# The transposes of the convolution's state, moved behind the first two weight tiles' products in two dense stages

## The reference, cut to what matters

```python
def conv_ffn(xn, prev, w_up, w_gate, conv_w, conv_b, w_down):
    h = xn @ w_up
    g = xn @ w_gate
    hp = jnp.concatenate([prev.astype(h.dtype), h], axis=1)
    hc = lax.conv_general_dilated(hp, conv_w.astype(hp.dtype)[:, None, :], window_strides=(1,), padding='VALID',
                                  dimension_numbers=('NWC', 'WIO', 'NWC'), feature_group_count=D_FF) + conv_b
    return (jax.nn.gelu(hc) * g) @ w_down, hp[:, -(CONV_W - 1):]
```

## Time and profile before

| | us |
|---|---|
| median of 3 runs (lowest to highest) | 3202.26 (3201.84 to 3204.47) |
| the profiled execution, its own time | 3207.11 |
| span of the profiled execution | 3205.3 |
| PE busy | 2954.8 (92% of the span) |
| DVE busy | 1442.0 (45%) |
| ACT busy | 944.4 (29%) |
| POOL busy | 742.1 (23%) |

### The profile page before, as it was taken

One profiled execution on the slowest core, in us unless ns is written; L12 is line 12 of the kernel. 1 busy time (PEld: TensorE's weight loads), 2 busy tenths in 40 slices (PEclk: granted clock), 3 DMA queues, 4 the chain that ended last, 5 costly groups with the idle time before them and its releaser, 6 DMA issues. The chain is left out here.

```text
span 3205.3 us, 51177 instructions
## 1 busy us (share of the span) xinstructions
PE 2954.8 (92%) x19701; PEld 2833.1 (88%) x19701; DVE 1442.0 (45%) x3259; ACT 944.4 (29%) x1692; POOL 742.1 (23%) x526
## 2 busy tenths in 40 slices
PE   7988996759999799999999999989789999999998
PEld 6987886449998499999999999968689999999998
DVE  4517773446776344431442443157644441441441
ACT  4213444335554132110211123047432110210211
POOL 1124552002111132221221224232132222221221
PEclk9998998757999899999999999979889999999999
DMA  6223552032000521111111111110021111111112
GB/s 175 80 86 114 158 158 63 1 71 108 2 1 23 242 63 40 46 46 46 46 48 44 52 42 44 41 42 1 14 63 34 52 46 46 46 46 46 46 48 72
DMA packets 270117, 195.93 MB, mean 61 GB/s; under 512 B 56388, under 2 KB 260286, under 8 KB 263407
## 3 DMA queue, kind: packets, MB, share of 16 engines
q1 hardware_dynamic: 262859, 143.19, 15.7%
q0 software_dynamic: 6912, 50.33, 4.4%
q10 hardware_dynamic: 184, 0.20, 0.0%
HBM read 176.64 MB, written 24.42 MB: 63 GB/s over the span
## 5 line engine op out<-in xcount | busy, mean ns | idle before, releaser
L590 PE MATMUL ps<-xf_hi,w_hi 128*128 128x344 f32 x2352 | 757.8, 322 | 9.9 <-POOL w_lo L581 9.9
L592 PE MATMUL ps<-xf_hi,w_lo 128*128 128x344 f32 x2352 | 754.3, 321 | 0.0
L591 PE MATMUL ps<-xf_lo,w_hi 128*128 128x344 f32 x2352 | 753.6, 320 | 0.0
L581 POOL TENSOR_TENSOR w_lo<-w_raw,w_hi 128x1024 fp32r<-128x1024 f32 (+1 forms) x162 | 384.9, 2376 | 1471.9 <-ACT w_hi L577 1471.9
L590 PEld LDWEIGHTS ps<-xf_hi,w_hi 128*128 128x128 f32 x2352 | 444.0, 189 | 11.3 <-issue 11.2
L591 PEld LDWEIGHTS ps<-xf_lo,w_hi 128*128 128x128 f32 x2352 | 443.9, 189 | 0.7 <-issue 0.7
L592 PEld LDWEIGHTS ps<-xf_hi,w_lo 128*128 128x128 f32 x2352 | 444.1, 189 | 0.0
L590 PE MATMUL ps<-hid_hi,w_hi 128*128 128x344 f32 x1056 | 339.8, 322 | 0.0
L592 PE MATMUL ps<-hid_hi,w_lo 128*128 128x344 f32 x1056 | 338.0, 320 | 0.0
L591 PE MATMUL ps<-hid_lo,w_hi 128*128 128x344 f32 x1056 | 337.3, 319 | 0.0
L577 ACT CAST w_hi<-w_raw 128x1024 fp32r<-128x1024 f32 (+1 forms) x162 | 165.6, 1022 | 388.8 <-PE ps L592 384.0
(11 more groups left out here) (565 smaller groups left out, 5381.8 us busy)
## 6 DMA issues: line engine op xcount, KB each, us to landing
w_raw<-in_ffn_w_up_dram SPq DMA_DIRECT2D x44, 512.0 KB, 3.7
w_raw<-in_ffn_w_gate_dram SPq DMA_DIRECT2D x44, 512.0 KB
w_raw<-in_ffn_w_down_dram SPq DMA_DIRECT2D x32, 448.0 KB, 3.5
w_raw<-in_ffn_w_down_dram SPq DMA_DIRECT2D x16, 512.0 KB, 3.6
w_raw<-in_a_w_in_dram SPq DMA_DIRECT2D x14, 512.0 KB, 3.8
w_raw<-in_c_w_in_dram SPq DMA_DIRECT2D x10, 512.0 KB, 3.9
residual<-hT SPq DMA_DIRECT2D x1, 4128.0 KB
hT<-residual SPq DMA_DIRECT2D x1, 4128.0 KB, 17.3
```

The lines of the kernel that those rows point to most:

```text
L581: pool.tensor_tensor(self.parts.lo[:, slot, 0:kt, :], self.raw[:, slot, 0:kt, :], self.parts.hi[:, slot, 0:kt, :].bitcast(F32), ALU.subtra ...
L590: pe.matmul(psum, w_hi, x_hi, start=(a == 0), stop=False)
L591: pe.matmul(psum, w_hi, x_lo, start=False, stop=False)
L592: ins = pe.matmul(psum, w_lo, x_hi, start=False, stop=(a == kt - 1))
```

## The change

The wait for `state_rows` and the 22 transposes leave their place ahead of job 0 on PE and stand behind job 1, ahead of job 2. The other engines' programs keep every row and every wait. From there on the line numbers of the kernel after are two higher (L965 is L967 there), and the transposes are L775.

```diff
-            pe.wait_ge(s_state, 16)
-            for f in range(KF):
-                ins = pe.transpose(k.ps[:, 6, f * 16:(f + 1) * 16], state_rows[:, f * P:(f + 1) * P], k.ident[0:16, 0:16])
-            ins.then_inc(s_stp, 1)
             for j in range(KD):
                 job(j, j % 2, os, KD, (s_ol, KD, KD) if j == 0 else None)
+                if j == 1:
+                    pe.wait_ge(s_state, 16)
+                    for f in range(KF):
+                        ins = pe.transpose(k.ps[:, 6, f * 16:(f + 1) * 16], state_rows[:, f * P:(f + 1) * P],
+                                           k.ident[0:16, 0:16])
+                    ins.then_inc(s_stp, 1)
```

## The result

The changed kernel took 3215.36 us (median of 7 runs, 3211.79 to 3222.89), the kernel before 3201.84 us (7 runs, 3196.80 to 3204.47): slower by 0.46%, ratio 1.0046 with a 95% interval of 1.0036 to 1.0057, which is 11.5 to 18.3 us. The profiled execution took 3214.49 us. Forecast were 3220.5 us and a range from 3213 to 3226.

The account below looks back on a forecast made before the run. PE was taken to set the pace in the dense stages, other engines hidden behind it. Head -3.28, transposes +2.5, wait +14.2, clock +4.8 gave +18.2 us on 3202.26: 3220.5 us, range 3213 to 3226.

Parts of the forecast that it names:

- The wait: Ahead of job 2: DVE's copy waits for the moved transposes, so PE waits 7.1 us a layer, 14.2 in all.
- The head: Start of the dense stages: job 0 starts 2.48 and 0.80 us earlier without transposes ahead, 3.28 us gained.
- a rise that had stayed in time: Head of the stages: if the clock rose at the same time as before, the gain would be 1.8 us.
- The transposes: Behind job 1, at the high clock: 1.26 us a layer on PE's path, 2.5 us in all.
- halving: Transposes behind job 1: their 2.52 us at the low clock level halved to 1.26 us a layer.
- The clock: Behind the new pause: job 2 starts at the low level, products 0.287 us apart, 4.8 us lost in all.
- The second rival: Ahead of job 2: the pause comes but the clock doesn't fall, 13.4 us slower, 3215.7 us; 10%.
- the third: Job 2 runs wholly at the low level, 9.4 us a layer in place of 2.4, 3234 us; 5%.
- The first rival: Ahead of job 2: the chain stays hidden beside job 1, only the head's gain is left, some 3201.5 us; 3%.
- the chain: From transposes' end through DVE's copy, additions, ACT's parts and POOL's low part to PE's job 2: 7.1 us a layer.
- The sum: Whole kernel: -3.28 + 2.5 + 14.2 + 4.8 = +18.2 us, to 3220.5 us, 0.57% slower.
- DVE's idle time: DVE idle between its last `os_lo` and the copy of the state for some 15 us.

Follow-up runs that it names:

- the wait alone: Kernel before, transposes still at the head; only DVE waits for job 1's last product ahead of its copy of the state: 3216.76 us, ratio 1.0052.
- the pause filled: Changed kernel with 36 more products into an unused bank behind the transposes, ahead of job 2: 3212.79 us, ratio 1.0031.
- the head filled: Kernel before with transposes behind job 0, 7 or 10 fp32 products ahead of it, and 28 products in the up tile's pause: 3196.99 us, ratio 0.9981.

## Why the prediction was right

**The wait.** The step on which all hung, that DVE's copy takes job 0's additions behind job 1 and so tile 2's weights out of job 1's shade, is shown three ways: the wait alone makes the pause, the copy moved behind the additions unmakes it, and the transposes moved one job earlier unmake it too. Its size was 6.67 us a layer against 7.1, at the lower end of what the prediction allowed. The difference is in the rows: the three hand-offs, transposes to copy, `xf_hi` to `xf_lo` and POOL to PE, took 0.03 or 0.04 us each in place of 0.14, and POOL's low part 2.35 us in place of the 2.46 of the earlier trace rows.

**The head.** 2.57 and 0.89 us against 2.48 and 0.80: right, and larger by the same short hand-off. The low stretch that followed was 6.19 and 4.40 us in the change, against 4.7 and 5.9 before by the same measure (first product to the first one that is short again). That the two sums are the same is luck in part: the second profile of the change had 3.9 and 4.4, the other two of before 5.0 and 5.0, and 3.5 and 5.0. The means, 4.7 and 4.9 us, speak for a gain that was whole, as chosen; a rise that had stayed in time would have made the stretches 1.7 us longer on the mean. The kernel without transposes agrees.

**The transposes.** 1.53 us in the trace for 22, some 1.6 with the start behind job 1's last product, against 1.26 by halving. Two starts in the trace are 0.062 us apart at the high level and 0.107 at the low: it is not a half, and the rest is at the ends of the row. The estimate of 2.35 us by the Trainium skill ("TensorE: Matmul & The Clock Gate", LDWEIGHTS: columns over 1.2) was the farther one at the high level; at the low level the trace agrees with it, 22 x 0.107 = 2.35 us between starts and 2.52 for the whole row.

**The clock.** It fell in the pause, as expected. The low stretches behind it were 3.04 and 5.55 us in the first profile, 5.03 and 5.56 in the second, against 4.9 and 5.6: 3.9 or 4.8 us lost where 4.8 were counted. The second rival, a clock that doesn't fall, is out by the rows, and by them alone: its 3215.7 us lies within 1.1 us of both medians, 3215.36 and 3214.64, and the forecast of 3220.5 lies 5 to 6 us above them. The products 0.287 us apart behind the pause decide, and the 1.4 and 1.6 us that the stages lost with the pause filled; the third, a job 2 wholly at the low level (72 x 0.287 = 20.7 us), is out by the rows, too. The first rival would need the chain hidden, which only the two kernels did that undo the wait.

**The sum.** By the profiles 17.6 us in the stages, with +18.2 forecast; by the runs 14.7 and 12.2, with intervals that reach to 18.3 and 16.3. The forecast's size is at the upper end. That the range held the time owes something to its width: the prediction took 2.6 us as the spread of runs, from three, where 23 runs of before spread over 18. The terms that were too large are the chain (0.9 us in both layers) and, in one profile, the clock (0.9); the transposes were too small by 0.7. And the sum had no term for the low stretch behind the up tile's pause, which came out shorter in these profiles, by 1.2 us of time. The rest of the difference between forecast and runs isn't traced to a row.

**DVE's idle time** was put at some 15 us and was 18.3 and 17.5.

## What to carry to other kernels

Ahead of moving work on one engine, look at what stands behind its consumer in another engine's program: here one copy on an in-order queue stood ahead of all additions, and the additions were what freed the banks, and what ACT's program waited for before it rounded the next weights. A chain that is hidden has a length (here 6.7 us) and a cover, the work of PE that runs beside it (here job 1, 11.3 us). The move is free as long as the cover still lies ahead (one job earlier it did), and costs the whole chain, not the difference, once the cover is spent. When PE has a pause that can't be removed, products into an unused bank kept the clock up here; they paid where they ended before the pause did and nothing else was late next.

## What the runs showed of the hardware

PE's clock fell during 88 transposes that ran without a break: granted clock 1.00, 0.69, 0.50 and 0.50 in four stretches of 2 us in layer 0, PE busy 2.00, 2.00, 2.00 and 1.87 us of them, and in layer 1 it fell some 2 us later. The Trainium skill ("TensorE: Matmul & The Clock Gate", Part 4) says that transposes don't bring the full clock about as matmuls do; these rows are in line with it, and add that they don't hold it. That it's the transposing, and not the small size of these instructions, isn't shown: ahead of layer 0's dense stage in the kernel before, PE was busy throughout with products of four columns that are no transposes (`sel_pT`, L3089), and the clock stayed at 0.50:

```profile
1109.80:1119.20 9.40, 9.39 (x177) 9.30 (x176) 0.00 (x0) 0.00 (x0) 0.00 (x0) 0.50 0.01 3
```

The stretch at the low level behind a restart differs from one to the next with the same work: over all these profiles from 2.95 to 6.19 us. With 0.287 us a product there against 0.157, that is up to 1.5 us of difference at each restart, and each execution has six of them in the changed kernel's dense stages.

A VectorE instruction that reads two SBUF tensors, begun beside one of POOL's low parts, didn't end before that part did. DVE's `os_lo` in the kernel with the head filled, four instructions, took 1.79 us ahead of POOL's first low part and 3.69 us from beside its start on, and one of the four makes the difference: it took 2.41 us where the others took 0.50, and ended 0.37 us behind POOL. An addition, one of whose tensors lies in PSUM, kept its 0.51 us beside POOL (the last two rows, from the kernel with the transposes behind job 0):

```profile
1123.24 2.37 POOL L581 TENSOR_TENSOR w_lo<-w_raw,w_hi 128x1024 fp32r<-128x1024 f32 x1 [48.02 <-ACT w_hi L577]
...
1123.57 2.41 DVE L969 TENSOR_TENSOR os_lo<-qT,os_hi 128x344 fp32r<-128x344 f32 x1 [1.71 <-ACT os_hi L860]
...
1150.48 2.40 POOL L581 TENSOR_TENSOR w_lo<-w_raw,w_hi 128x1024 fp32r<-128x1024 f32 x1 [7.02 <-ACT w_hi L577]
...
1152.11 0.51 DVE L904 TENSOR_TENSOR hT<-hT,ps 128x344 f32<-128x344 f32 x1 [2.77 <-PE ps L592]
```

Over the 13 profiles, 81 instructions of `os_lo` and `xf_lo` began while a low part had over 0.6 us to go; all ended 0.37 or 0.38 us behind it, and 325 additions begun likewise took 0.51 or 0.52 us. No run took POOL's work away, but the ends follow POOL's in every case. A PE at the high level at the head runs into that.
